# An attention stage with eight heads: the head loop written out, and the products of weights and values given out to the steps anew

## What is computed

```python
def diff_attn_branch(h, w_in, w_out, ...):
    proj = h @ w_in
    q, k, v, z = jnp.split(proj, 4, axis=-1)      # 8 heads, two maps of 64 each, values 128 wide
    ...
    def block(start):                              # 128 query rows
        s = jnp.einsum('bhmqd,bhmkd->bhmqk', qb, k) * scale
        s = s - (slopes[:, None, None] * dist)[None, :, None]
        p = jax.nn.softmax(s, axis=-1)
        pd = p[:, :, 0] - lam * p[:, :, 1]
        return jnp.einsum('bhqk,bhkv->bhqv', pd, v)
```

## Time and profile before

| | us |
|---|---|
| median of three runs | 3018.04 |
| profiled execution | 3023.28 |
| its span | 3021.5 |
| TensorE matmul busy in the span | 2846.3 (94%) |
| VectorE busy | 1836.8 (61%) |
| ScalarE busy | 1734.3 (57%) |
| GpSimd busy | 1637.9 (54%) |
| attention stage, about | 812 to 2106 of the span |

### The profile page before, as it was taken

The page is one execution under the profiler, slowest core; times in us unless marked ns, Lnnn a source line. Parts: engine busy times, 40 slices in busy tenths (PEclk is TensorE's granted clock), DMA queues, the critical chain, the costliest instruction groups (busy, mean ns, idle before and its releaser), DMA issues. The chain is left out here.

```text
span 3021.5 us, 44677 instructions
## 1 busy us (share of the span) xinstructions
PE 2846.3 (94%) x15098; PEld 2498.6 (83%) x15098; DVE 1836.8 (61%) x2402; ACT 1734.3 (57%) x3126; POOL 1637.9 (54%) x1060
## 2 busy tenths in 40 slices
PE   3999999999899999999999999998899899899899
PEld 3899999999878788878787878886688899887687
DVE  7668766865477776767776777776886200341322
ACT  4667776776477777767777777775443321222321
POOL 5888764654266565656565666565664221130642
PEclk8999999999999999999999999999999999999899
DMA  2655464367344414131322232121664522565752
GB/s 84 194 162 175 146 178 138 120 177 202 103 116 150 107 33 102 36 97 46 77 66 71 64 79 64 36 90 40 215 209 148 206 89 76 150 177 181 264 182 104
DMA packets 281846, 374.32 MB, mean 124 GB/s; under 512 B 22923, under 2 KB 258507, under 8 KB 276140
## 3 DMA queue, kind: packets, MB, share of 16 engines
q1 hardware_dynamic: 279404, 369.14, 40.2%
q10 hardware_dynamic: 2080, 2.10, 0.2%
q0 software_dynamic: 128, 0.13, 0.0%
HBM read 258.04 MB, written 125.97 MB: 127 GB/s over the span
## 5 line engine op out<-in xcount | busy, mean ns | idle before, releaser
L1272 DVE TENSOR_REDUCE pa_half_max<-pa_score 128x1 f32<-128x1024 f32 x512 | 625.9, 1223 | 334.9 <-PE pa_score L1056 333.9
L1206 ACT ACTIVATE pa_p<-pa_score,pa_neg_max 128x1024 f32<-128x1024 f32 x512 | 567.9, 1111 | 71.4 <-DVE pa_neg_max L1278 71.3
L206 PE MATMUL ia_acc<-ia_xh,ia_wh 128*128 128x384 f32 x1344 | 461.9, 344 | 76.1 <-DVE ia_xl L686 43.4
L1117 PE MATMUL pa_o_acc<-pa_wt,pa_vv 128*128 128x256 f32 x2048 | 512.7, 381 | 1.8 <-ACT pa_o_out_s L1241 1.6
L1052 PE MATMUL pa_score<-pa_ka,pa_qa 128*128 128x512 f32 x1024 | 456.0, 445 | 19.3 <-ACT pa_p L1206 8.1
L1184 ACT ACTIVATE pa_wt<-pa_turned 128x512 f32<-128x512 f32 x512 | 306.5, 599 | 270.7 <-PE pa_turned L1086 269.2
L207 PE MATMUL ia_acc<-ia_xl,ia_wh 128*128 128x384 f32 x1344 | 458.1, 341 | 0.0
L208 PE MATMUL ia_acc<-ia_xh,ia_wl 128*128 128x384 f32 x1344 | 457.9, 341 | 0.0
L443 POOL TENSOR_TENSOR ia_w_sums<-ia_raw 128x512 f32<-128x512 f32 x240 | 334.6, 1402 | 177.8 <-PE ia_acc L208 159.8
L1056 PE MATMUL pa_score<-pa_kb,pa_qb 96*128 96x512 f32 x1024 | 422.9, 413 | 0.0
L1117 PEld LDWEIGHTS pa_o_acc<-pa_wt,pa_vv 128*128 128x128 f32 x2048 | 367.4, 191 | 47.5 <-ACT pa_o_out_s L1241 2.7
(11 more groups left out here) (284 smaller groups left out, 5340.1 us busy)
## 6 DMA issues: line engine op xcount, KB each, us to landing
ia_raw<-attn_w_in SPq DMA_DIRECT2D x46, 1024.0 KB, 6.7
qk_hi<-ia_hi SPq DMA_DIRECT2D x96, 192.0 KB, 3.1
qk_lo<-ia_c SPq DMA_DIRECT2D x96, 192.0 KB, 2.9
pa_ka<-qk_hi SPq DMA_DIRECT2D x32, 512.0 KB, 6.4
fl_slices<-normed SPq DMA_DIRECT2D x26, 512.0 KB, 6.5
ia_h<-x_cols SPq DMA_DIRECT2D x24, 384.0 KB, 6.3
v<-ia_c SPq DMA_DIRECT2D x48, 192.0 KB, 6.1
attn_gate<-ia_c SPq DMA_DIRECT2D x48, 192.0 KB, 1.9
```

The source lines that it names most:

```text
L206: pe.matmul(out, a_hi(k), b_hi(k), start=first and n == 0, stop=False)
L1117: mm = pe.matmul(o_acc[:], vv[:, k], wt[:, g % 2, k], start=k == 0, stop=k == NB - 1)
L1206: act.activation(dst[:, half * HALF:(half + 1) * HALF], score[:, (4 * q + j) % RING].rearrange("p a b -> p (a b)"), ACT.Exp, bias=neg_max[ ...
L1272: dve.tensor_reduce(half_max[:, q % 2, n, half:half + 1], score[:, (4 * q + j) % RING].rearrange("p a b -> p (a b)"), AX_X, ALU.max).then_ ...
```

## The change

It has three parts, all in `attend`. First, the hardware loop goes: `run` writes all eight heads out, so semaphore values and addresses are constants. Second, `product_at` and `OUT_AT` give way to a table QUARTERS, which says for each step how many key blocks P0 to P3 hold. The stream of all 130 blocks of a head is cut by it. The numbers of blocks are: step 4: 6 (2, 2, 1, 1); steps 5 to 14: 8; step 15: 7; step 16: 11 (3, 3, 3, 2); steps 0 and 1 of the next head: 8; step 2: 6 (2, 2, 1, 1); step 3: 4, which are the last two blocks of pair 7 in P0 and the sample's product in P1. So pair g begins in P1 of step 2g+4 (pair 0 in P0) and ends in P0 of step 2g+6; pair 5 ends in P0 of step 16, pair 6 in P3 of step 0, pair 7 in P0 of step 3. A pair that ends in P0 is copied out by ScalarE between take T0 and take T1 of the same step, in the sample step before take T0; pair 6 and the sample are copied at the start of steps 1 and 4. SyncE stores a pair in the step after the one in which it ended; pair 7 is stored with the sample in step 4. Third, the sample step has an order of its own on TensorE: h0 P0 h1 T0 P1 T1 P2 T2 P3 T3, where it was h0 h1 T0 P0 T1 P1 T2 T3 P2 P3. The waits of a pair on the turned weights become finer: one for every four key blocks.

```diff
-        OUT_AT = {1: (NP - 2, 1), 3: (NP - 1, 1), 4: (NP, 1), **{2 * g + 6: (g, 0) for g in range(NP - 2)}}
+        QUARTERS = {4: (2, 2, 1, 1), **{q: (2, 2, 2, 2) for q in range(5, NB - 1)}, NB - 1: (2, 2, 2, 1),
+                    NB: (3, 3, 3, 2), 0: (2, 2, 2, 2), 1: (2, 2, 2, 2), 2: (2, 2, 1, 1), 3: (2, 2, 0, 0)}
...
         def run(eng, step):
-            for q in range(STEPS):
-                step(0, 0, q)
-            with eng.Fori(0, HEADS // 2 - 1) as j:
-                for s in range(2):
-                    for q in range(STEPS):
-                        step(2 * j + 1 + s, 1 - s, q)
-            for q in range(STEPS):
-                step(HEADS - 1, 1, q)
+            for h in range(HEADS):
+                for q in range(STEPS):
+                    step(h, h % 2, q)
...
+                    for g, k, back in products_of[q][quarter]:
+                        acc = o_acc[:]
+                        if k == 0:
                             wait(pe, o_copied, OUTS * (h - back) + g)
...
+                            if k % 4 == 0:
+                                t, kind, c = last_turn(g, k // 4)
+                                late = back and 2 * g + 3 < STEPS
+                                pe.wait_ge(turned_out, unit(h, t, kind, c) + 1 - (UNITS if late else 0))
...
+                    if q == SAMPLE:
+                        half(0)
+                        pair(0)
+                        half(1)
+                        for c in range(NC):
+                            turn(c)
+                            if c < NC - 1:
+                                pair(c + 1)
...
+                    copy_out(None)
...
+                    if q == SAMPLE:
+                        copy_out(0)
                     take(0)
...
+                    if q != SAMPLE:
+                        copy_out(0)
                     take(1)
...
                     exp(0)
+                    copy_out(1)
                     take(2)
```

More of the change, by code:

```diff
@@ L896, in turned_block, with last_turn @@
             return (t - 2) % STEPS
[L898 to L906, removed]
-        OUT_AT = {1: (NP - 2, 1), 3: (NP - 1, 1), 4: (NP, 1), **{2 * g + 6: (g, 0) for g in range(NP - 2)}}
+        QUARTERS = {4: (2, 2, 1, 1), **{q: (2, 2, 2, 2) for q in range(5, NB - 1)}, NB - 1: (2, 2, 2, 1),
+                    NB: (3, 3, 3, 2), 0: (2, 2, 2, 2), 1: (2, 2, 2, 2), 2: (2, 2, 1, 1), 3: (2, 2, 0, 0)}
+        BLOCKS = {q: sum(sizes) for q, sizes in QUARTERS.items()}
+        stream = [(g, k) for g in range(NP) for k in range(NB)] + [(NP, 0), (NP, 1)]
+        products_of, out_of, copied_at, begun = {}, {}, {}, 0
+        for q, n in BLOCKS.items():
+            taken = [(g, k, 1 if q < 4 else 0) for g, k in stream[begun:begun + n]]
+            begun += n
+            sizes = QUARTERS[q]
+            assert sum(sizes) == n
+            products_of[q] = [taken[sum(sizes[:x]):sum(sizes[:x + 1])] for x in range(4)]
+            for x, part in enumerate(products_of[q]):
+                for g, k, back in part:
+                    if k == (1 if g == NP else NB - 1):
+                        assert (g, k, back) == part[-1] and (x != 2 or g == NP)
+                        after = (q + 1) % STEPS
+                        if x < 2 and g < NP:
+                            copied_at[(q, x)] = g, back
+                        else:
+                            copied_at[(after, None)] = g, 1 if after <= 4 else 0
+                        out_of.setdefault(after, []).append((g, 1 if after <= 4 else 0))
+        assert begun == len(stream)
+        def last_turn(g, c):
+            turn = ((2 * g + 3) % STEPS, "w", c)
+            return max(turn, (1 + c, "v", c), key=lambda x: place[x]) if g == 0 else turn
         def is_first(h):
@@ L924, in step_parts @@
                         pairs=not (first and q < 4) and (scored or q < 4),
[L925 removed]
+                        out=q in out_of and not (first and q < 6) and (scored or q < 5))
         def run(eng, step):
[L928 to L935 removed]
+            for h in range(HEADS):
+                for q in range(STEPS):
+                    step(h, h % 2, q)
             for q in range(5):
@@ L990, in step @@
                         load_q(h, nxt) if nxt < NP else load_q(h + 1, 0)
-                    if parts["out"]:
-                        g, back = OUT_AT[q]
+                    for g, back in out_of[q] if parts["out"] else ():
                         hold(sp, sp_held, o_copied, OUTS * (h - back) + g + 1)
@@ L1232, in exp, with copy_out @@
                             exponential_sample(h, j)
-                    if parts["out"]:
-                        g, back = OUT_AT[q]
+                    def copy_out(x):
+                        if (q, x) not in copied_at:
+                            return
+                        g, back = copied_at[(q, x)]
+                        if is_first(h) and back or is_past(h) and not back:
+                            return
                         act.wait_ge(pair_done, OUTS * (h - back) + g + 1)
```

51 lines of the change are left out of this document (21 added, 30 removed).

## The result

The changed kernel takes 2995.06 us, the median of four runs (2993.71 to 3001.8), where the kernel before has 3017.81 us beside it (3015.02 to 3025.29): a ratio of 0.9925, 95% interval 0.9902 to 0.9948. In a second comparison it was 0.9925 again (0.991 to 0.994). The forecast was -10.7 us, and it came to -22.8. The direction was right, the forecast was less than half of it, and the time lies outside the range.

The account below looks back on a forecast made before the run. Attention was taken as paced by TensorE's instruction stream; -0.82 us in each of heads 1 to 7, -0.7 in head 0 and -4.2 for the edges made -10.7 us: 3018.04 to 3007.3 us, range 3001 to 3014.

Parts of the forecast that it names:

- What bounds the kernel: Attention stage: paced by TensorE's instruction stream, busy 1255 of 1294 us; a part gains only what it takes from TensorE's waits.
- The loop: Two back edges of the head loop: writing the heads out removes both gaps, -4.2 us.
- That the parts add up: Whole change: edges and per-head terms costed separately and summed to -10.6 us, -10.7 with rounding.
- my -6.5 for the rest: All terms but the loop's edges: what the change would still gain if the loop gave nothing, -6.5 us.
- The sample step: Step 16 of each head: the new order removes TensorE's waits, 1.16 us a head, -9.3 us for eight heads.
- 0.94 for T3: Sample step: T3, directly behind T2, starts late because ScalarE takes T2 late; 0.94 us a head gained.
- Steps 2 to 4: Blocks given away make V wait 0.63 us, costing 0.44 a head; step 3 to P0 of step 4 gains 0.1.
- from H3 on all stands as it did: Step 3: H3 starts where it stood, its wait of 0.46 us filled with work, and later waits stay unchanged.
- The waits of steps 1 to 5 go too: Rival: V and P0 of step 4 come on time, another 7.6 us go, step 4 loses nothing; 2996 us, 7%.
- The loop gives nothing: Rival: the edge gaps return in straight code or have another cause; -6.5 us, 3011.5 us, 12%.
- the sample step gives half: Rival: its wait moves to T3 or the following H0 and T0; -6 us, 3012 us, 14%.
- the slow copy: Rival: the mid-step copy on ScalarE delays 40 steps; slower from 0.67 us delay each, some 3031 us at 1 us; 7%.

Follow-up runs that it names:

- pe_one_trip: Kernel before, TensorE's loop holding heads 1 to 6 in its body and running once; ratio 0.9957.
- pe_padded: Kernel before, loops kept, 13,300 already-met waits appended to TensorE's attention code (1.99 MB); executed once, attention begins at 804.7 us.
- flat_only: Kernel before with all eight heads written out on every engine and nothing else; ratio 0.9931.
- pe_flat: Kernel before with the head loop written out on TensorE alone; ratio 0.9948.
- loop_kept: Changed kernel with the hardware loop over the heads put back, new table and order kept; ratio 0.9994.
- turn3_after_p2: Kernel before, loop kept, with T3 behind P2 instead of ahead of it in the sample step; ratio 0.9984.
- flat_turn3: Kernel before with the head loop written out on all engines and T3 behind P2 in the sample step; ratio 0.9926.
- six_in_three: Changed kernel with the six blocks of steps 2 and 4 as (2, 2, 2, 0) instead of (2, 2, 1, 1); 2990.36 us, ratio 0.989.
- pe_two_trips: Kernel before with TensorE looping over heads 3 to 6 only, two trips, the other heads written out (1.79 MB); ratio 0.9954.

## Why the prediction was right or wrong

**What bounds the kernel: wrong as a limit on the gain.** The step that failed is "a part of the change gains only what it takes out of TensorE's waits", said of attention. It holds within the stage, and I took it for the whole program. The first stage gave 7.6 us in this pair of traces and 9.7 in the mean over both kinds, with none of its instructions touched. No row of before could have shown it. What the prediction could have had is a bound: every part had been costed only where its instructions stand, and a program that grows by a quarter on one engine was a change of its own, left without a term. Of the 11 us by which the sum was short in the spans, this is 7.6. That TensorE's longer code is what shortens the stage is shown by pe_one_trip and pe_padded; by what path it does so stays open.

**The loop: right.** Forecast -4.2, measured 1292.3 - 1296.3 = -4.0 in flat_only, and pe_flat shows that it is TensorE's loop alone. The Trainium skill has in "Advanced Engine Details and Errata", section "Control Flow Timing", a taken branch at about 51 ns; the measured edge is 2 us, and up to 6 us of a head in loop_kept, so the measurement decides against it as a price. The mechanism stands in the Trainium skill, "Runtime: NRT & Kernel Launch", section "Instruction fetch mechanics": a taken branch whose target isn't in the window of instructions at hand makes the sequencer fetch it before it can go on, while straight code is fetched ahead. The traces agree with both halves: at each of the 13 backward edges a 16 KB packet of TensorE's program starts 0.9 to 1.6 us after the last waiting instruction and lands before H0, and straight code has such packets without idle time. That section gives no price for the stall; here it is 3.9 to 4.6 us from T3 to H0, 5.5 once. The prediction had taken the whole 4.2 from the trace and needed no mechanism for it.

**That the parts add up: wrong, though it did no harm in the sum.** I costed sample step and edges one by one. They interact: loop_kept has the shorter heads and loses all of it at two edges, because T3 as the last instruction leaves nothing queued across the branch. Had the loop stayed, my -6.5 for the rest would have been 0. In the changed kernel there are no edges, so the sum wasn't touched.

**The sample step: right mechanism, undersized.** All of its waits went, as forecast. VectorE's maxima give steps 15, 16 and the next 0, one with another, 1.37 us less for the same blocks, where I had 1.16. The largest single term, 0.94 for T3, was exact (turn3_after_p2). What I had left out is small: h1 waited too, about 0.1, and T3 was not late behind P3, where I had allowed 0 to 0.05.

**Steps 2 to 4: right in each wait, too dear in the sum.** V of step 2 waits 0.63, H3 of step 3 waits no more, P0 of step 4 waits as before: all three as written. V of step 3 waits 0.19 more, which "from H3 on all stands as it did" had wrong, and still the three steps cost 0.15 a head where I had 0.44 - 0.1 = 0.34. By VectorE's maxima most of the difference lies in step 2, which is 0.5 to 0.6 us shorter where 0.43 were forecast; why wasn't followed up. A head was thus forecast at 157.0 - 0.82 = 156.1 and takes 155.8; eight times the difference of 0.3 to 0.4 are 3 us, the rest of the miss in attention. The copy in the middle of the step cost nothing, as forecast: all heads from the second on take 155.8.

**The rivals.** "The waits of steps 1 to 5 go too" named 2996 us, almost the time measured, and is wrong: V of step 3 and P0 of step 4 wait in after as before. A right number by a wrong mechanism. "The loop gives nothing" and "the sample step gives half" are refuted by flat_only and flat_turn3, the slow copy by the heads of 155.8.

**The worth of the table.** flat_turn3 reaches the changed kernel's attention time with one exchange. Table and new order are worth 0.3 us a head beyond it, too little to be told in the times; with the blocks of steps 2 and 4 set right (six_in_three) they are worth 1.2.

## What to carry to other kernels

Cost an edit where its instructions stand, and then ask once more what the whole program becomes: when code grows or shrinks, compare first the stages that weren't touched, before any of the gain is put down to the edit. At a loop's backward edge keep work queued behind the engine's last wait, or, more surely, write out the loop of the engine that bounds the stage, and of that engine alone: with the same four blocks queued the edges of these runs cost 2 to 3 us each, and the one of pe_two_trips 7. When a block must be given away in a step, give away the one behind the next wait, not the one that covers it.

## What the runs showed of the hardware

- A backward branch of TensorE's loop (a body of two heads) left it idle for 1.5 to 2.2 us with four blocks queued behind the last wait (nine edges, one of them with a second gap of 2.49), 3.0 with two (two edges) and 3.5 and 4.87 with none. Straight code of the same instructions had no such gap in any head.
- At each of these 13 edges a packet of 16 KB on the queue of TensorE's program started 0.9 to 1.6 us after the last waiting instruction and took 1.0 to 1.6 us (2.3 once, beside another); the first matmul came 1.65 to 2.3 us after its end.
- After 4.87 us of idleness the clock was granted at 0.50 (1.2 GHz) for the next 4.5 us, and the score matmuls started every 0.43 us instead of 0.23. A gap of 3.50 was followed by 0.79 on average over 3 us. Of eight edges with gaps of 1.5 to 2.2 us three were followed by a stretch at 0.50.
- With TensorE's code at 1.79 to 1.99 MB instead of 1.57, packets of 1 KB in the first stage took 56 to 60 ns on average instead of 65 (the median is 46 in both; packets over 100 ns were 4.7 to 6.8% instead of 9.9%), and the stage was 4 to 15 us shorter. This held whether the extra code was heads or empty waits, run or not yet run. The cause is open.
- The code of the other engines, looped or not, made no difference that these runs can tell.
